# A streaming attention layer in float32: bounds amid the projections, both heads' values in one pass of 64-column strips

## What is computed

```python
def fox_attend(q, k, v, cq, ck, q_pos, k_pos):
    s = jnp.einsum('bqhd,bkhd->bhqk', q, k, preferred_element_type=jnp.float32) * ATTN_SCALE
    s = s + jnp.transpose(cq, (0, 2, 1))[:, :, :, None] - jnp.transpose(ck, (0, 2, 1))[:, :, None, :]
    mask = k_pos[None, :] <= q_pos[:, None]
    s = jnp.where(mask[None, None], s, -jnp.inf)
    p = jax.nn.softmax(s, axis=-1).astype(v.dtype)
    return jnp.einsum('bhqk,bkhd->bqhd', p, v)
```

## Time and profile before

| | us |
|---|---|
| median of 3 runs | 1530.82 |
| lowest and highest | 1530.29, 1531.12 |
| the profiled execution | 1526.91 |
| span of its instructions | 1525.2 |
| PE busy | 1423.7 (93%) |
| DVE busy | 735.3 (48%) |
| ACT busy | 421.4 (28%) |

### The profile page before, as it was taken

One profiled execution on the slowest core, in us unless ns is written; L12 is line 12 of the kernel. 1 busy time (PEld: TensorE's weight loads), 2 busy tenths in 40 slices (PEclk: granted clock), 3 DMA queues, 4 the chain that ended last, 5 costly groups with the idle time before them and its releaser, 6 DMA issues.

```text
span 1525.2 us, 19242 instructions
## 1 busy us (share of the span) xinstructions
PE 1423.7 (93%) x7499; PEld 1232.9 (81%) x7499; DVE 735.3 (48%) x1186; ACT 421.4 (28%) x741; POOL 83.2 (5%) x119
## 2 busy tenths in 40 slices
PE   4979989899898993998999999999999999999997
PEld 3765967859677882887989998999889988999896
DVE  6355364453634646675444454444444444444444
ACT  5124233242334546231312211221112211221110
POOL 2510101101000000000000000000000000000000
PEclk8989999999999996999999999999999999999999
DMA  6023432514222112111111110111011110111004
GB/s 186 8 69 91 127 79 68 143 44 120 65 75 68 30 57 94 60 42 47 60 32 55 41 41 28 55 55 41 19 50 55 41 41 28 55 41 44 24 28 125
DMA packets 133130, 92.87 MB, mean 61 GB/s; under 512 B 22358, under 2 KB 122710, under 8 KB 133076
## 3 DMA queue, kind: packets, MB, share of 16 engines
q1 hardware_dynamic: 133076, 92.14, 21.2%
HBM read 78.24 MB, written 9.68 MB: 58 GB/s over the span
## 4 chain that ended last, share of the span: by engine, by line
PE 88%; DVE 6%; ACT 2%; issue 1%; DMA 1%; POOL 1%; SPq 1%; ACTq 0%; DVEq 0%
PE psum L1473 25%; PE psum L1474 25%; PE psum L1475 25%; PE psum L1694 4%; PE psum L1678 1%; PE psum L1650 1%; DVE tops L1207 1%; PE psum L1681 1%; PE psum L1539 1%; PE psum L1772 1%; POOL rs L694 1%; PE psum L1586 1%; PE psum L1561 1%; DVE cross_qk L1199 0%; PE psum L1793 0%
## 5 line engine op out<-in xcount | busy, mean ns | idle before, releaser
L1441 DVE TENSOR_TENSOR mix<-psum,mix 128x512 f32<-128x512 f32 x288 | 196.4, 690 | 160.4 <-PE psum L1475 160.3
L1473 PE MATMUL psum<-h_hi,wu_hi 128*128 128x384 f32 x768 | 258.9, 337 | 4.2 <-DVE mix L1395 4.2
L1474 PE MATMUL psum<-h_lo,wu_hi 128*128 128x384 f32 x768 | 258.6, 337 | 0.0
L1475 PE MATMUL psum<-h_hi,wu_lo 128*128 128x384 f32 x768 | 258.6, 337 | 0.0
L1473 PE MATMUL psum<-wd_hi,u_hi 128*128 128x512 f32 x576 | 224.2, 389 | 3.6 <-issue 3.6
L1474 PE MATMUL psum<-wd_lo,u_hi 128*128 128x512 f32 x576 | 224.1, 389 | 0.0
L1475 PE MATMUL psum<-wd_hi,u_lo 128*128 128x512 f32 x576 | 224.1, 389 | 0.0
L1473 PEld LDWEIGHTS psum<-h_hi,wu_hi 128*128 128x128 f32 x768 | 144.9, 189 | 4.9 <-issue 4.4
L1474 PEld LDWEIGHTS psum<-h_lo,wu_hi 128*128 128x128 f32 x768 | 144.8, 189 | 0.5
L1475 PEld LDWEIGHTS psum<-h_hi,wu_lo 128*128 128x128 f32 x768 | 144.8, 189 | 0.0
L985 ACT CAST wd_hi<-raw 128x1024 fp32r<-128x1024 f32 x32 | 32.1, 1049 | 401.3 <-PE psum L1475 399.9
(11 more groups left out here) (257 smaller groups left out, 2137.3 us busy)
## 6 DMA issues: line engine op xcount, KB each, us to landing
raw<-in_w_up_dram SPq DMA_DIRECT2D x32, 512.0 KB, 4.6
raw<-in_w_down_dram SPq DMA_DIRECT2D x32, 512.0 KB, 3.3
k_c<-in_cache_k_dram SPq DMA_DIRECT2D x32, 256.0 KB, 3.0
raw<-in_w_in_dram SPq DMA_DIRECT2D x32, 192.0 KB, 4.1
out_dram<-mix SPq DMA_DIRECT2D x9, 512.0 KB
x_in<-in_x_prompt_dram SPq DMA_DIRECT2D x8, 512.0 KB, 4.0
v_c<-in_cache_v_dram SPq DMA_DIRECT2D x16, 256.0 KB, 4.9
kts<-in_cache_v_dram SPq DMA_DIRECT2D x16, 256.0 KB, 3.8
```

The lines of the kernel that those rows point to most:

```text
L1441: nc.vector.tensor_tensor(at, psum[:, 4 + 2 * (t % 2) + half, :].rearrange("p (k n) -> p k n", n=P), at, ALU.add).then_inc(y_added, 1)
L1473: nc.tensor.matmul(out, hi(k), r_hi(k), start=first and k == 0, stop=False)
L1474: nc.tensor.matmul(out, hi(k), r_lo(k), start=False, stop=False)
L1475: last = nc.tensor.matmul(out, lo(k), r_hi(k), start=False, stop=end and k == n - 1)
```

## The change

- The order of the steps: heads alternate, s % 2 is the head. `values(u)` now does both heads of one key tile: two matmuls, one with 64 columns of values into PSUM rows 0 to 63, the other into rows 64 to 127 of the same bank. `v1` has no ones any more.
- `weight_sums` makes the sums of four steps (two key tiles, two heads): four matmuls with 32 columns of ones (`ones_s`) into four strips of 32 rows of a bank, six times a pair. `denominators` copies them, and DVE adds odd and even key tiles in `invert`.
- `pt` has six buffers, in the space of the past values; past values of streams 0 to 3 are therefore loaded when the pair's last sums are done. `exp` waits for the sums of the buffer's last use.
- `project` has four quarters, and `amid` places bounds and a turn between those of tiles 6, 7 and 8; bounds (0,4) and (0,5) use banks 2 and 3. `BOUND_ORDER` is DVE's order, `BOUND_AFTER` the maximum that frees the bank.
- `high` for tiles 4 to 7 works on two tiles at a time, behind projections 6 to 8. `outputs` copies both heads at once. `share_out` stands behind DVE's copy of the second stream's keys. The store of values is one transfer.

```diff
 def attention_step(s):
-    if s < 8:
-        return s // 4, 0, s % 4
-    return (s - 8) // 8, 1, (s - 8) % 8
+    return (s % 2, 0, s // 2) if s < 8 else (s % 2, 1, (s - 8) // 2)
...
-    pt = sb(over, "pt", [P, 3, SPAN])
+    pt = sb(over, "pt", [P, 6, SPAN])
...
+    BOUND_ORDER = [("b", 0, 0), ("b", 0, 1), ("b", 0, 2), ("b", 0, 3), ("s", 0, 0),
+                   ("b", 1, 0), ("b", 1, 1), ("b", 1, 2), ("b", 1, 3), ("b", 0, 4), ("s", 1, 0),
+                   ("b", 1, 4), ("b", 0, 5), ("b", 1, 5), ("b", 0, 6), ("b", 1, 6), ("b", 0, 7), ("b", 1, 7),
+                   ("s", 0, 1), ("s", 1, 1)]
...
     def bound_bank(hp, t):
-        return 6 + (5 * hp + t) % 2 if t < 4 else 6
+        if t < 4:
+            return 6 + (5 * hp + t) % 2
+        return 2 if (hp, t) in ((0, 4), (0, 5)) else 6
...
                 for b in range(2, 6):
                     sp.wait_ge(kc_turned, DEC_B * p + b - 1)
                     past_keys(p, b)
+                sp.wait_ge(den_done, 6 * p + 6)
+                past_values(p, 0)
                 if not last:
-                    sp.wait_ge(st_done, STEPS * (p + 1))
                     decay_rows(p + 1)
...
+                    for part in range(4):
+                        last = split_product(
+                            psum[:, 4 + t % 2, 0:PW3],
+                            lambda k: h_hi[:, 2 * part + k, tile(t)], lambda k: h_lo[:, 2 * part + k, tile(t)],
+                            lambda k: wp_hi[:, 2 * part + k, :], lambda k: wp_lo[:, 2 * part + k, :], 2, part == 0, part == 3)
+                        if part < 3:
+                            amid(t, part)
...
+                    for hp in range(2):
+                        r = head_rows(hp)
+                        last = nc.tensor.matmul(psum[r, 4 if qc == 0 else 0, a0 - qc * SPAN:SPAN], v1[:, kt, r],
+                                                pt[:, (s + hp) % 6, 0:a1 - a0], start=kt == 0, stop=kt == 4 * qc + 3)
+                    last.then_inc(pv_done, 1)
+
+                def weight_sums(kt_of):
+
+                    for i in range(4):
+                        s = 2 * kt_of + i
+                        _, qc, kt = attention_step(s)
+                        a0, a1 = step_queries(s)
+                        last = nc.tensor.matmul(psum[32 * i:32 * i + 32, 5 if qc == 0 else 1, a0 - qc * SPAN:SPAN], ones_s[:],
+                                                pt[:, s % 6, 0:a1 - a0], start=kt < 2, stop=kt >= 4 * qc + 2)
+                    last.then_inc(den_done, 1)
...
+                def amid(t, quarter):
+                    if (t, quarter) == (6, 1):
+                        bound(0, 2)
+                        bound(0, 3)
+                    if (t, quarter) == (7, 1):
+                        bound(1, 1)
+                        bound(1, 2)
+                    if (t, quarter) == (7, 2):
+                        bound(1, 3)
+                        bound(0, 4)
+                    if (t, quarter) == (8, 1):
+                        bound(1, 4)
+                        bound(0, 5)
+                    if (t, quarter) == (8, 2):
+                        turn_qk(7)
...
                 scores(0)
-                bound(1, 3)
-                turn_tops(1, 0)
-                bound(0, 4)
-                for s in range(STEPS):
-                    if s < STEPS - 1:
-                        scores(s + 1)
-                    values(s)
...
+                scores(1)
+                bound(1, 5)
+                meanwhile = {0: (0, 6), 1: (1, 6), 2: (0, 7)}
+                for u in range(STEPS // 2):
+                    if u == 3:
+                        bound(1, 7)
+                    if u < STEPS // 2 - 1 and u != 3:
+                        scores(2 * u + 2)
+                        scores(2 * u + 3)
+                    values(u)
+                    if u % 2 == 1:
+                        weight_sums(u - 1)
+                    if u in meanwhile:
+                        bound(*meanwhile[u])
+                    if u == 3:
                         turn_qk(NT - 1)
                         turn_tops(0, 1)
                         turn_tops(1, 1)
+                        scores(8)
+                        scores(9)
+                    if u in (8, 9, 10):
+                        turn_past(p, u - 8)
+                turn_past(p, 3)
```

More of the change, by code:

```diff
@@ L163, in streaming_step @@
     tops = sb(pair, "tops", [P, 2, NT - 1])
-    dens = sb(pair, "dens", [P, SPAN])
+    dens = sb(pair, "dens", [P, 2, SPAN])
     top = sb(pair, "top", [P, 2])
@@ L168, in streaming_step @@
     rden = sb(pair, "rden", [P, 2])
-    o_own = sb(pair, "o_own", [P, 2, P])
     pair.close()
@@ L846, in pair_act @@
                 if p == 0:
                     act.wait_ge(c_past_ready, 1)
-                high(4, 0)
-                exp(0)
-                high(4, 1)
-                for s in range(1, 6):
+                high(6, 2, 1)
+                for s in range(8):
                     exp(s)
-                outputs(0, 0)
                 act.wait_ge(qk_turned, NT * p + NT)
                 nc.scalar.activation(q_own[:], psum[:, 0, 0:P], ACT.Copy, scale=qgain[:, 0:1]).then_inc(hi_done, 1)
-                for s in range(6, STEPS):
+                for s in range(8, STEPS):
@@ L1226, in pair_dve @@
                         samples_meanwhile(p - 1, t)
-                    mean(t)
+                    if t == 5:
+                        if p == 0:
+                            dve.wait_ge(consts_ready, 3)
+                            dve.wait_ge(stored, 16 * NT)
+                        low(0, 0)
+                        low(0, 1)
+                    if t == 6:
+                        bound(0, 2)
+                        bound(0, 3)
+                    if t == 7:
+                        bound(1, 1)
+                        bound(1, 2)
+                        bound(1, 3)
+                        bound(0, 4)
+                    if t == 8:
+                        bound(1, 4)
+                        bound(0, 5)
+                    mean(t)
+                    if t == 5:
+                        bound(0, 0)
+                        bound(0, 1)
+                    if t == 6:
+                        shift(0, 0)
+                    if t == 7:
+                        shift(1, 0)
+                    if t == 8:
+                        bound(1, 5)
                     norm(t)
+                    if t == 6:
+                        bound(1, 0)
                     if p == 0 and t == 2:
@@ L1612, in pair_pe, with project @@
             def pair_pe(p):
-                def project(t):
+                def project(t, amid):
                     if t >= 2:
@@ L1680, in scores, with values @@
                         nc.tensor.matmul(psum[:, 2 + s % 2, 0:P], cmask[:], ident_b[:], start=False, stop=False)
-                    nc.tensor.matmul(out, KB[:, hp, tile(kt)], QB[:, hp, a0:a1], start=False, stop=True).then_inc(st_done, 1)
-                def values(s):
-                    hp, qc, kt = attention_step(s)
+                    nc.tensor.matmul(out, cross_qk[:, kt // 4, 1, hp, tile(kt % 4)],
+                                     cross_qk[:, qc, 0, hp, a0 - qc * SPAN:a1 - qc * SPAN],
+                                     start=False, stop=True).then_inc(st_done, 1)
+                def values(kt_of):
+                    s = 2 * kt_of
+                    _, qc, kt = attention_step(s)
                     a0, a1 = step_queries(s)
```

265 lines of the change are left out of this document (120 added, 145 removed).

## The result

The changed kernel takes 1532.51 us (median of 20 runs, 1529.49 to 1537.19), the kernel before 1530.44 us beside it (1527.2 to 1532.14). The ratio is 1.0016, 95% interval 1.0009 to 1.0023: slower by 2 us, which is less than the 3 us that the prediction called hard to tell from no change. Forecast were 1521 us and a range of 1509 to 1531. The expected gain of 9.5 us did not come.

A forecast was written before the change was run, and what follows sets the result against it. TensorE, busy 93% of the span, was taken to bound the kernel. Stretch A -5.9, B -8.0, last pair's queue +0.4 and clock +4 made -9.5 us: 1517 profiled, 1521 for the median, range 1509 to 1531.

The forecast's parts named there:

- stretch A: From the end of the sixth projection to the second query block's first score; forecast 33.4 us, -5.9 us in all.
- B: From stretch A's end through the transposes of past keys behind attention; forecast 24.5 us from 26.5, -8.0 us in all.
- The bounds amid projections: Six bounds moved ahead of the ninth projection's end: projections end at 300.8, first value product at 304.1, new wait 0.7 us.
- Halves run together: Value products of both heads, 64 columns each, run side by side: 7.7 us a pair instead of 15.3.
- the rival in turn: At the value products the second half waits for the first: 1546 us; chance 0.12, shared with visits at twice 0.3.
- A visit at 0.3: Each of twelve turns a pair from whole-array products into strips and out costs 0.3 us on PE.
- free visits: Going into strips and out costs nothing: B gains 3.0 us a pair, 1509 us; chance 0.08.
- The clock: Half clock around the lull before the second block: 2 us on two pairs, +4; in every pair as rival, 0.17.
- with half as many turns to value products, each with two exps' lead, I keep 1.7 of it: In B, of 2.9 us in boundaries and short waits for exps, 1.7 stays: -1.2 us a pair.
- Those are wanted behind two turns and a projection of 4.26 us: Past-value loads ahead of two loads of keys at attention's end cost nothing, the keys being wanted some 7 us off.
- That is 9.8 us: In stretch A, DVE's chain from the maximum of (0,6) at 305.9 to the shift; second block's scores start at 315.8.
- The terms of the strips: Per pair, -3.4 us for values and sums and +4.5 for visits and inner steps; strips by themselves lose 1.1.

The follow-up runs named there:

- The run with the bounds behind: The fastest kernel with the bounds and turn between quarters of the last three projections issued behind each projection instead; 1506.67 us, 0.9854 of the kernel before.
- the fastest kernel: The changed kernel with early bounds, spread turns of past keys, loads of values last, and fewer visits with four score banks; 1501.11 us, 0.9809 of the kernel before.
- the run with the loads of values last: The changed kernel with the four loads of past values moved behind the last two loads of keys on SyncE's queue; 1526.98 us, 0.9979.
- the kernels with and without strips: The changed kernel with early bounds and spread turns of past keys, with its strips or with them undone; 1507.62 us against 1508.07.
- the kernels with early bounds: The changed kernel with the last four bounds and turns of tops earlier on PE, the second split halved on DVE; alone 1518.07 us, 0.9921.
- the exchanged split: The changed kernel with the maximum of (0,7) put ahead of the second split of block two on DVE; 1531.41 us, 1.0013.

## Why the prediction was wrong

By the profiled executions the forecast was 9.5 us of gain; the changed kernel's profile is 1.1 us longer from the start of pair one's stretch A (87.14 before, 88.03 now) to the gate products behind the pairs (478.75 and 480.71). Of the 10.6 us between them the smallest part is in A: with its clock it was to save 1.9 us over the four pairs and saved 1.3. B was to save 8.0 and saved 0.4. What lies behind B was to lose 0.4 and lost 2.7.

**Right.** *The bounds amid projections*: projections end at the forecast time, the new wait at bound (1,2) is 0.67 for 0.7, the first value product is 0.1 us off. The run with the bounds behind shows that the place is worth 1.5 us a pair in the fastest kernel. *That DVE's chain then sets A, and that the waits ahead of bound (1,7) and for the shift are late next*: 1.96 and 0.76 us for 2 and 0.9. *Halves run together*: the second starts 0.01 us behind the first, and 512 queries take 1.01 us; the rival in turn is out. *A visit at 0.3*: 0.27 to 0.34; free visits are out. *The clock* came out by some luck: forecast were 2 us on each of two pairs; it fell in three, and cost 1.3, 1.3 and 0.8 in A and 0.9 at the start of B in the fourth, 4.3 for 4.

**The failed steps**, in us over the four pairs:

- "*with half as many turns to value products, each with two exps' lead, I keep 1.7 of it*": the walk of B followed PE and gave the exps their lead, but did not follow ACT's own order. Behind exp 21 ACT has a copy that waits for PE's third turn of keys, at 338.28, and exps 22 and 23 stand behind that copy. The last value product, which now needs both, waits 1.03 us in each pair: 4.1. The run with the copy moved took it away.
- "*Those are wanted behind two turns and a projection of 4.26 us*", "*some 7 us off*", by which the four loads of past values cost nothing: the last load of keys is issued at 345.34 and wanted at 349.8, 4.5 us later and not 7, and behind 1 MB it takes 4.7 us. The seventh and eighth turns wait: 1.1, 1.1 and 0.4 us in three pairs by the lengths of the rest, about 3, where 0 stood. Moved behind the keys they gave 2.7 us by the lengths and 5.5 by the medians. The price for a lost cover that the prediction names, up to 3 us a pair, was the right place to look.
- "*That is 9.8 us*", of DVE's chain, and A of 33.4: at full clock the chain is 10.4 us (pair one) and A 34.0 (pair three of the run with the loads of values last), 0.6 us more than forecast. Bound (1,7) took 0.9 for 0.7, and each hand-over between PE and DVE adds some hundredths that the sum had left out. 4 x 0.6, about 2.
- *The sixth load of keys* waited 0.41 to 0.55 for 0.5, as forecast.

4.1 + 3 + 2 make 9 of the 10.6; the rest is not placed. With the first two undone and no wait for keys B is 24.18; with the forecast 0.5 for the sixth load it would be 24.7, against 24.5. The terms of the strips, -3.4 and +4.5, did less harm than the prediction gave them: in B, where they were to lose 0.4 us a pair, the kernels with and without strips are even, and in A, where DVE's chain was to hide them, whole products make PE later with its bounds and strips save 0.4. So strips as the change has them save 0 to 0.5 us a pair where 1.1 of loss stood. The Trainium skill's rule (TensorEngine Tiling (Array Packing), "Key Properties") that a change of mode drains the engine agrees with the price of 0.3 for a visit; undoing every strip all the same gained nothing.

## What to carry to other kernels

When an order is rewritten on one engine, walk the queues of the others too: the two dearest misses here were a copy ahead of two exps on ACT and four loads ahead of two on SyncE, each harmless in the old order. For a load, count the cover from its issue to its use, and add the time of what is in flight ahead of it. A stretch with several short waits on one engine is one chain: order what is on its path (bounds ahead of products, half a split in each gap) rather than shorten one wait; here this gave 14 us, and shortening one wait gave 0.5, within its error. Compare stretches only at equal clock: one order took 33.99 or 35.27 us here by the clock alone. Products in strips are worth having in runs: pay the way in and out once for several.

## What the runs showed of the hardware

Strips and the full array: 0.27 to 0.34 us from whole-array products into strips and back, at 2.4 GHz; read in the rows it is 0.10 on the pass ahead, 0.15 on the passes inside and 0.10 on the first pass behind; going on from 64 to 32 columns costs what the last pass pays on the way out anyway (1.01 us from values to the sums, 323.78 to 324.79, as to a score, 321.59 to 322.60), some 0.1 where 0.15 was forecast.

The clock: in pairs two to four of the kernels with early bounds, whose waits in A are at most 0.7 us and apart, the granted clock is 1.00 throughout; with 1.3, 0.7 and 0.8 us within a few us of each other (the exchanged split) it went to half (0.50) behind the last. But short waits do not decide it alone: with 2.0 and 0.8 us the changed kernel fell to half there in pairs two to four and not in pair one, the run with the loads of values last did not in pair three, and the kernel with bounds behind stayed at 1.00 in pairs two to four with waits of 1.2 and 0.7.

The last stage: PE pauses 3.58 us near the end in both kernels (until 1495.81 and 1496.55), with no releaser in the trace. Windows behind it, of the kernel before and of the changed one:

```profile
1500.00:1505.00 5.00, 5.00 (x24) 4.14 (x23) 2.77 (x4) 0.00 (x0) 0.00 (x0) 1.00 0.67 194
```

```profile
1500.00:1505.00 5.00, 5.00 (x19) 3.98 (x19) 1.66 (x4) 0.00 (x0) 0.00 (x0) 0.79 0.17 52
```

Same pause, but the clock fell behind it in one execution and not in the other; of the eleven profiles of the experiments ten have it at half there. This makes 2.6 of the 3.3 us between the two profiled spans, and it is no part of the change: ahead of it the two were 0.74 us apart. Two single profiles say little about 2 us; the medians and the lengths of stretches say more. What makes the pause was not tried.
